# Gated attention in high and low parts: three split passes in place of fp32 products, and two output products issued earlier

## The reference, cut to what matters

```
def gla_scan(q, k, v, lg):
    def step(s, inp):
        qc, kc, vc, gc = inp
        cum = jnp.cumsum(gc, axis=1)
        qg = qc * jnp.exp(cum)
        kg = kc * jnp.exp(-cum)
        att = jnp.where(causal, jnp.einsum('blhk,bshk->bhls', qg, kg), 0.0)
        o = jnp.einsum('bhls,bshv->blhv', att, vc) + jnp.einsum('blhk,bhkv->blhv', qg, s)
        kd = kc * jnp.exp(cum[:, -1:] - cum)
        s = s * jnp.exp(cum[:, -1])[..., None] + jnp.einsum('bshk,bshv->bhkv', kd, vc)
        return s, o

    o = gla_scan(q, k, v, lg[:, :, 0]) + rev(gla_scan(rev(q), rev(k), rev(v), rev(lg[:, :, 1])))
    o = rmsnorm(o, onorm).reshape(bsz, seq, D_INNER) * jax.nn.silu(z.astype(f32))
```

## Time and profile before

| | before |
|---|---|
| median of 3 runs | 2014.81 us |
| lowest, highest | 2013.41, 2014.96 us |
| span of the profiled execution | 2012.7 us |
| mean granted clock of TensorE | 0.999 |
| busy TensorE / VectorE / ScalarE / GpSimd | 1994.2 / 1053.4 / 958.9 / 1199.7 us |
| from DRAM | 95 GB/s over the span |

### The profile page before, as it was taken

One profiled execution on the slowest core, in us unless ns is written; L12 is line 12 of the kernel. 1 busy time (PEld: TensorE's weight loads), 2 busy tenths in 40 slices (PEclk: granted clock), 3 DMA queues, 4 the chain that ended last, 5 costly groups with the idle time before them and its releaser, 6 DMA issues.

```text
span 2012.7 us, 27974 instructions
## 1 busy us (share of the span) xinstructions
PE 1994.2 (99%) x10644; PEld 1672.5 (83%) x10644; DVE 1053.4 (52%) x1576; ACT 958.9 (48%) x1641; POOL 1199.7 (60%) x955
## 2 busy tenths in 40 slices
PE   9999999999999999999999999999999999999998
PEld 7888899988877788899888779988897887777787
DVE  3184677642144436587632388778875244443321
ACT  4124445622244446355523386677675335554543
POOL 4445888875542225889865568788886442423342
PEclk9999999999999999999999999999999999999999
DMA  5233332333433312323333343434433421212131
GB/s 172 85 103 98 102 105 85 110 90 93 120 102 87 94 51 84 105 85 105 107 93 100 104 126 109 126 105 111 129 96 85 107 89 63 65 62 84 42 105 63
DMA packets 259573, 193.66 MB, mean 96 GB/s; under 512 B 9555, under 2 KB 247431, under 8 KB 259448
## 3 DMA queue, kind: packets, MB, share of 16 engines
q1 hardware_dynamic: 256188, 190.67, 31.8%
q10 hardware_dynamic: 3260, 1.28, 0.3%
HBM read 189.66 MB, written 2.27 MB: 95 GB/s over the span
## 4 chain that ended last, share of the span: by engine, by line
PE 57%; issue 23%; POOL 15%; ACT 2%; DVE 2%; DMA 1%; POOLq 0%; SPq 0%; ACTq 0%; DVEq 0%
POOL wlo L813 13%; PE bank L2624 12%; PE bank L2625 12%; PE bank L2626 12%; PE bank L2850 5%; PE bank L2851 5%; PE bank L2852 5%; PE bank L3232 1%; PE bank L3228 1%; PE bank L3196 1%; POOL f0aLo L849 1%; DMA rows<-cums 1%; DVE xc L2207 1%; POOL wlo L882 0%; DVE xC L2207 0%
## 5 line engine op out<-in xcount | busy, mean ns | idle before, releaser
L813 POOL TENSOR_TENSOR wlo<-raw,whi 128x512 fp32r<-128x512 f32 (+1 forms) x532 | 673.3, 1297 | 696.4 <-ACT whi L971 682.8
L971 ACT ACTIVATE whi<-raw 128x2048 fp32r<-128x2048 f32 (+1 forms) x131 | 233.0, 1779 | 306.9 <-PE bank L2626 298.2
L2624 PE MATMUL bank<-hHi,whi 128*128 128x512 f32 (+1 forms) x880 | 349.7, 397 | 1.0 <-DVE hLo L2535 0.9
L2626 PE MATMUL bank<-hHi,wlo 128*128 128x512 f32 (+1 forms) x880 | 341.5, 388 | 0.0
L2625 PE MATMUL bank<-hLo,whi 128*128 128x512 f32 (+1 forms) x880 | 341.2, 388 | 0.0
L2624 PE MATMUL bank<-whi,hHi 128*128 128x256 f32 (+1 forms) x640 | 219.3, 343 | 0.4 <-issue 0.3
L2626 PE MATMUL bank<-whi,hLo 128*128 128x256 f32 (+1 forms) x640 | 208.5, 326 | 0.0
L2625 PE MATMUL bank<-wlo,hHi 128*128 128x256 f32 (+1 forms) x640 | 208.3, 325 | 0.0
L834 POOL TENSOR_TENSOR wlo<-raw,whi 128x512 fp32r<-128x512 f32 x134 | 196.0, 1489 | 17.3 <-ACT whi L1138 17.3
L2624 PEld LDWEIGHTS bank<-hHi,whi 128*128 128x128 f32 x880 | 165.3, 188 | 40.8 <-issue 5.1
L2626 PEld LDWEIGHTS bank<-hHi,wlo 128*128 128x128 f32 x880 | 165.3, 188 | 34.7
(11 more groups left out here) (490 smaller groups left out, 4408.9 us busy)
## 6 DMA issues: line engine op xcount, KB each, us to landing
raw<-in_ssd_w_in SPq DMA_DIRECT2D x48, 512.0 KB, 5.0
raw<-in_ffn_w_gate SPq DMA_DIRECT2D x44, 512.0 KB, 4.8
raw<-in_ffn_w_up SPq DMA_DIRECT2D x44, 512.0 KB, 4.8
raw<-in_gla_w_in SPq DMA_DIRECT2D x40, 512.0 KB, 4.5
rows<-cums SPq DMA_DIRECT2D x64, 256.0 KB, 5.5
raw<-in_ffn_w_down SPq DMA_DIRECT2D x32, 384.0 KB, 3.4
raw<-in_attn_w_qkv SPq DMA_DIRECT2D x24, 512.0 KB, 4.3
raw<-in_conv_w_in SPq DMA_DIRECT2D x23, 512.0 KB, 4.4
```

What stands on the lines that cost most here:

```text
L813: ins = pool.tensor_tensor(wlo[s][:, part], raw[s][:, part], whi[s][:, part].bitcast(F32), ALU.subtract)
L971: act.activation(whi[s][:, 0:w], raw[s][:, 0:w], ACT.Copy).then_inc(w_hi, 1)
L2624: pe.matmul(dst, hi1, hi2, start=first, stop=False)
L2626: return pe.matmul(dst, lo1, hi2, start=False, stop=last)
```

## The change

The values, the turned keys and the attention weights are now kept as a high and a low part each, of type F32R, and their products are three split passes (`product`) instead of one fp32 product.

- Values: ScalarE's copy writes the high part `gvHi` (semaphore `gv_hi`, a used-up one under another name), and VectorE's new `value_low` subtracts it from the bank into `gvLo`; now VectorE frees the bank. There is one set of four tiles for all heads instead of two, so ScalarE's copy waits until the previous head's products have read the tile (`values_read`).
- Turned keys: ScalarE writes `kdHi0` and `kdHi1`, VectorE's new `keys_low` writes `kdLo`, and the increments wait for it (`kd_lo`).
- Attention weights: a cast to `attHi` and a subtraction into `attLo` on VectorE at the end of `attention`.
- `outs(h, 0)` goes ahead of the second half of piece 0. `outs(h, 1)` goes to the end of piece 0 in heads 1 and 2 and stays in piece 1 in heads 0 and 3. ScalarE's `keep` follows them, and VectorE's `states(h, 2)` goes to piece 0.
- `t32` has another place in memory, and the scratch for DMA descriptors is set to 1024.

```diff
--- before.py
+++ after.py
@@ -174,7 +174,8 @@
 
 LATER = {"q_hi": ("x_turn", 8), "q_lo": ("w0_lo", 3), "q_mm": ("y_mixed", 8), "s_made": ("y_hi", 8), "kept": ("x_squared", 8),
          "c_made": ("w0_hi", 1), "xg_made": ("cu_edge", 1), "t_made": ("rb_one", 1), "t_hi": ("toe_mm", 2), "t_lo": ("y_ready", 8),
-         "f_hi": ("x_in0", 16), "f_lo0": ("x_in1", 16), "f_lo1": ("x_in2", 16)}
+         "f_hi": ("x_in0", 16), "f_lo0": ("x_in1", 16), "f_lo1": ("x_in2", 16),
+         "gv_hi": ("vec_ready", 3), "kd_lo": ("vec_turned", 4)}
 
 
 STAGES = ["conv", "ffn0", "attn", "ffn1", "mid", "ssd", "gla", "end"]
@@ -262,9 +263,6 @@
         rc = sb("rc", [P, 24 * 8])
         stat = sb("stat", [P, 64])
         m_g45 = sb("g45", [P, 64])
-        t32 = [sb(f"t32_{i}", [P, SEQ]) for i in range(2)]
-
-
         @contextmanager
         def scope(spec):
             with ExitStack() as c:
@@ -275,6 +273,8 @@
                 return m
 
         R8, R4, V = [P, KT * SEQ], [P, NT * SEQ], [P, SEQ]
+        m_keys = area([(f"kdHi{d}", V, F32R) for d in range(2)])
+        t32 = [sb(f"t32_{i}", [P, SEQ]) for i in range(2)]
         m_in = area([("xtok", R8, F32), ("vrows", [P, 3 * P], F32), ("xsq", R8, F32)])
         m_conv = area([("cu", [P, KT * 514], F32), ("c0", V, F32), ("c1", V, F32), ("r2", V, F32), ("cacc", [P, 2 * SEQ], F32),
                        ("yHi", R8, F32R), ("yLo", R8, F32R)])
@@ -310,8 +310,8 @@
         with scope([("gO", [P, NT * DI], F32)]) as m_go:
             m_gl = area([("wgl4", [P, KT * P], F32R)])
             m_gla = area([("gst", [P, 6 * SEQ], F32), ("gQK", [P, 8 * SEQ], F32), ("lg", [P, 2 * SEQ], F32),
-                          ("kg", [P, 2 * SEQ], F32), ("diff", [P, 2 * SEQ], F32), ("att", V, F32), ("glT", V, F32R),
-                          ("gv0", R4, F32), ("gv1", R4, F32), ("wgf", [P, 1024], F32R),
+                          ("kg", [P, 2 * SEQ], F32), ("diff", [P, 2 * SEQ], F32), ("att", V, F32), ("attHi", V, F32R), ("attLo", V, F32R),
+                          ("glT", V, F32R), ("gvHi", R4, F32R), ("gvLo", R4, F32R), ("kdLo", [P, 2 * SEQ], F32R), ("wgf", [P, 1024], F32R),
                           ("attF", [P, P], F32), ("attB", [P, P], F32),
                           ("gdec", [P, 4 * NGC], F32), ("tdec", [P, 4 * NT], F32)])
             m_gla2 = area([("gHi", R8, F32R), ("gLo", R8, F32R)])
@@ -431,8 +431,21 @@
         def h4(ap):
             return ap.rearrange("p (h e) -> p h e", h=HPG)
 
-        def values(h, t):
-            return tile(m_gla[f"gv{h % 2}"], t)
+        def values(t):
+
+            return tile(m_gla["gvHi"], t), tile(m_gla["gvLo"], t)
+
+        def turned_keys_of(d, t):
+
+            return tile(m_keys[f"kdHi{d}"], t, P), m_gla["kdLo"][:, SEQ * d + P * t:SEQ * d + P * (t + 1)]
+
+        def attended(t):
+
+            return tile(m_gla["attHi"], t, P), tile(m_gla["attLo"], t, P)
+
+        def values_read(h, t):
+
+            return 8 * h + (2 if t in (0, NT - 1) else 4)
 
         def decayed_q(h, d):
 
@@ -1587,7 +1600,10 @@
 
                 def value_tile(h, t):
 
-                    copy(values(h, t), projected("v", h, t), S(f"side{t % 2}"), scale=rcol(5, t))
+                    v = projected("v", h, t)
+                    if h:
+                        act.wait_ge(S("go_mm"), values_read(h - 1, t))
+                    copy(values(t)[0], v, L("gv_hi"), scale=rcol(5, t))
 
                 def value_piece(h, p, half):
 
@@ -1649,7 +1665,7 @@
                 def turned_keys(h):
                     for d in range(2):
                         act.wait_ge(S("kd_turned"), 2 * h + d + 1)
-                        copy(t32[d][:, :], bank[6 + d][:, :], S("kdt_ready"))
+                        copy(m_keys[f"kdHi{d}"][:, :], bank[6 + d][:, :], S("kdt_ready"))
 
                 def keep(h, n):
 
@@ -1688,12 +1704,14 @@
                         if n == 3 and h < 3:
                             turned_keys(h + 1)
                         fill(h, n, 0)
+                        if n == 0:
+                            keep(h, 0)
                         fill(h, n, 1)
                         if h >= 2:
                             turned(h - 2, n)
-                        if n < 2:
-                            keep(h, n)
-                        else:
+                        if n == (1 if gla_piece(h, 0, 1) is None else 0):
+                            keep(h, 1)
+                        elif n >= 2:
                             squares(h, n)
                         if n == 0 and h < 3:
                             for d in range(2):
@@ -2490,7 +2508,22 @@
                         chain.note(dve.copy_predicated(m["attF"][:, :], LE[:, :].bitcast(I32), bank[4][:, P * t:P * (t + 1)]))
                         chain(dve.copy_predicated(m["attB"][:, :], GE[:, :].bitcast(I32), bank[5][:, P * t:P * (t + 1)]))
                         chain(tt(att[:, P * t:P * (t + 1)], m["attF"][:, :], m["attB"][:, :], ALU.add))
-                    dve.sem_inc(S("att_ready"), 1)
+                    chain(dve.tensor_copy(m["attHi"][:, :], att[:, :]))
+                    tt(m["attLo"][:, :], att[:, :], m["attHi"][:, :].bitcast(F32), ALU.subtract).then_inc(S("att_ready"), 1)
+
+                def value_low(h, t):
+
+                    dve.wait_ge(*late("gv_hi", 4 * h + t + 1))
+                    hi, lo = values(t)
+                    from_bank = (early_bank(t) if h == 0 else bank[t % 2])[:, :]
+                    stt3(lo, from_bank, rcol(5, t), hi.bitcast(F32), ALU.mult, ALU.subtract).then_inc(S(f"side{t % 2}"), 1)
+
+                def keys_low(h):
+
+                    for d in range(2):
+                        dve.wait_ge(S("kdt_ready"), 2 * h + d + 1)
+                        tt(m["kdLo"][:, SEQ * d:SEQ * (d + 1)], bank[6 + d][:, :], m_keys[f"kdHi{d}"][:, :].bitcast(F32),
+                           ALU.subtract).then_inc(L("kd_lo"), 1)
 
                 def states(h, n):
 
@@ -2528,6 +2561,9 @@
                     piece = gla_piece(h, n, e)
                     if piece and piece[0] == "z":
                         gate(*piece[1:])
+                    elif piece and piece[3]:
+                        for t in (2 * piece[2], 2 * piece[2] + 1):
+                            value_low(piece[1], t)
 
                 def y_low(k):
                     dve.wait_ge(S("gy_hi"), k + 1)
@@ -2542,12 +2578,12 @@
                             states(h, 1)
                             if h:
                                 head_mean(h - 1)
-                        elif n == 1:
-                            states(h, 2)
                         if n == 0 and h < 3:
                             cumulate(h + 1)
                         if n == 0 and h:
                             head_inverse(h - 1)
+                        if n == 0:
+                            states(h, 2)
                         fill(h, n, 0)
                         if n == 2 and h < 3:
                             spans(h + 1)
@@ -2557,6 +2593,8 @@
                         fill(h, n, 1)
                         if n == 1 and h < 3:
                             factors(h + 1)
+                        if n == 3 and h < 3:
+                            keys_low(h + 1)
                         if n >= 2 and (h or n == 3):
                             add(h, n)
 
@@ -2576,8 +2614,13 @@
                 q_or_k(7)
                 dve.wait_ge(S("gqk_free"), 8)
                 factors(0)
+                for t in range(2):
+                    value_low(0, t)
                 spans(0)
                 attention(0)
+                keys_low(0)
+                for t in range(2, NT):
+                    value_low(0, t)
                 for h in range(GLA_HEADS):
                     head(h)
                 head_mean(GLA_HEADS - 1)
@@ -3457,7 +3500,7 @@
                 def increments(h, n):
 
                     if n == 0:
-                        pe.wait_ge(S("kdt_ready"), 2 * h + 2)
+                        pe.wait_ge(*late("kd_lo", 2 * h + 2))
                         pe.wait_ge(S("att_ready"), h + 1)
                         for t in (2, 3):
                             pe.wait_ge(S(f"side{t % 2}"), SIDE["v", h, t][1] + 1)
@@ -3465,7 +3508,7 @@
                         pe.wait_ge(S("gla_state"), 6 * h + 2)
                     for d in range(2):
                         t = n if d == 0 else NT - 1 - n
-                        pe.matmul(bank[4 + 2 * d + n % 2][:, :], tile(t32[d], t, P), values(h, t), start=True, stop=True).then_inc(S("gu_mm"), 1)
+                        product(bank[4 + 2 * d + n % 2][:, :], *turned_keys_of(d, t), *values(t), True, True).then_inc(S("gu_mm"), 1)
 
                 def outs(h, n):
 
@@ -3479,7 +3522,7 @@
                         t = out_tile(n, d)
                         out = bank[2 + d]
                         if n < 2:
-                            ins = pe.matmul(out[:, :], m["att"][:, P * t:P * (t + 1)], values(h, t), start=True, stop=n == 0)
```

(9 more changed lines are left out.)

## The result

| | before | after |
|---|---|---|
| median of 5 runs | 2014.81 us | 2027.21 us |
| lowest, highest | 2013.41, 2015.18 us | 2026.7, 2028.29 us |
| span of the profiled execution | 2012.7 us | 2025.2 us |
| mean granted clock of TensorE | 0.999 | 0.996 |

The changed kernel is slower: the ratio is 1.0063, 95% interval 1.0051 to 1.0075. The forecast was 2026.7 us, with a range of 2019 to 2033.

What follows compares the result with a forecast made beforehand. TensorE, busy 99% of the span at full clock, was taken to bound the kernel. The passes' -7.1 and the added waits summed to +11.9 on 2012.7, span 2024.6, so 2026.7 us; range 2019 to 2033 at 0.8.

Steps and rivals of the forecast that it cites:

- The sum: All terms over the whole kernel: +11.9 us on the profiled span of 2012.7, giving 2024.6.
- Passes: On TensorE, 40 fp32 products of 0.858 become 120 passes of 0.227: 7.1 us less, 1.8 per head.
- Weight chain of head 1: TensorE waits for z's weight unit, late behind ScalarE's held copy of value tile 1: 3.5 to 4.6, taken as 4.1 us.
- Weight chain of head 2: Same chain plus one ScalarE copy, taken in two waits, 1.5 and about 2.9: together 4.4 us.
- The first part: In head 2, piece 1 waits 1.5 us for bank 0, which ScalarE's copy frees.
- Factors on VectorE: In heads 1 and 2, factor products slowed beside GpSimd's low parts make the scores late, 1.9 and 2.1; taken as 3.4 us.
- rival 1: Clock falls to 1.2 GHz in the two large waits, likelier about 2 us each: 2028 to 2033, chance 0.15.
- Tails: Between heads, VectorE's added casts and subtractions make TensorE wait: 1.3, 2.6, 0.7 and 0.8, with smaller waits at bank 0.
- Start of head 0: First increments wait for VectorE's added cast and subtractions: 1.3 us.
- Heads 1 to 2 and 2 to 3: First increments wait for the two key subtractions on VectorE: 0.7 and 0.8 us.
- turned(0, 2): In head 2, turning part 2 of head 0's outputs waits for bank 0, freed later by VectorE: 1.3 us.
- turned(0, 0): In head 2, turning part 0 of head 0's outputs waits for value tile 0's low part, behind the states: 0.3 us.

Runs made afterwards that it cites:

- e4: Changed kernel, each product of high and low parts as one fp32 matmul of the high parts, low parts made but unused: 2033.84 us, ratio 1.0097.
- e5: Changed kernel with a second pair of buffers for value tile 1 and output 1 back between the halves of the values' second piece: 2025.23 us, ratio 1.0054.
- e8: Changed kernel with ScalarE making the factors between the copies of value tiles 0 and 1 in heads 1 and 2: 2026.32 us, ratio 1.0058.
- e2: Changed kernel with VectorE's six factor products ahead of the low parts of value tiles 2 and 3 in heads 1 and 2: 2025.63 us, ratio 1.0059.
- e1: Changed kernel with 15 and 12 extra TensorE passes into unused bank 7 during the weight-unit waits of heads 1 and 2: 2026.64 us, ratio 1.006.
- e3: Changed kernel with the edits of e1 and e2 together: 2023.81 us, ratio 1.0048.
- e7: Changed kernel with the edits of e5, e6 and e2 together: 2018.9 us over 11 runs, ratio 1.0019.
- e11: e10 with the second key subtraction awaited only by the second increment, and head 2's step-2 states behind tile 0's low part: 2011.25 us, ratio 0.9984.
- e6: Changed kernel, VectorE's order between heads: attention-weight split behind key and value subtractions, key subtractions ahead of second z products in heads 1, 2: 2025.66 us, ratio 1.0053.
- e10: e7 with gate copies ahead of squares, addition ahead of split, head 2's bank-0 copy earlier, output 0 later, value tile 0 double-buffered: 2013.01 us, ratio 0.9991.

## Why the prediction came out right, and where it did not

The sum, +11.9, met +12.5 of span, and the passes and the two weight chains came in the size forecast. That it came so near is in part luck: it took 3.4 for a wait that is 0, and left out 4.4 of slow passes.

- **Passes, -7.1: right.** 0.227 apart in the products; head 3 alone gives 1.64 of its 1.78 back, and e4 prices a product at 0.18.
- **Weight chain of head 1, 4.1: right.** 3.55, by the chain counted: the held copy at 1745.13, keeps, table load, factors, high part at 1752.03, low part from 1754.01. e5 (chain taken away, wait gone) and e8 (factors taken out of it, 1.70 left, and that set by another chain) show it. VectorE's way through GpSimd's low part was a part of it: 0.43 (e2).
- **Weight chain of head 2, 4.4: size right, cause half wrong.** 1.42 + 2.81 = 4.2. The first part is as forecast. Of the second the unit makes 1.6; the rest is bank 0, which the prediction named but let be free at the same time. With output 1 ahead of turned(0, 1), nothing of TensorE's stands between this and z(1, 0) while ScalarE finishes a high part. It stands ahead of it in e5 too, which is one reason why e5 got so little.
- **Factors on VectorE, 3.4: the step that failed.** The contention was right (1.75 to 1.77 a product), the lateness too: with the clock held up the scores waited 1.67 and 1.17 (e1), against 1.9 and 2.1 (in head 3's factors only four of the six products were slow). The forecast counted with a wait of 4.6 for the unit in this step and with 4.1 in the sum; with 4.1 its own 1.9 would have been 2.4. But in the kernel after, that wait is 0. The clock fell, the first half of z took 2.7 and 1.7 longer, and the scores were wanted later. The 4.4 of rival 1 stood in the place of the 3.4, not on top: the rival's 2028 to 2033 added the two and was too high. e1 and e2, which each take one of them away, gain 0.8 and 1.8 in the two heads, and 1.1 of the 1.8 is that the clock was at half for a shorter time; e3, which takes both, gains 4.5.
- **Tails: right.** Start of head 0: 1.3 forecast, 1.75 measured, of which some 0.5 lie ahead of it (the last attention weight was done that much later). Head 0 took 41.45 where 40.69 - 1.78 would be left: 2.5 against 2.6. Heads 1 to 2 and 2 to 3: 0.55 and 0.58 against 0.7 and 0.8. turned(0, 2): 1.10 against 1.3. turned(0, 0), 0.3, has no wait.

What the chip did between VectorE and GpSimd was read from rows before and after alike. The Trainium skill, SBUF — State Buffer, "Summary: rules for kernel authors", has a VectorE instruction with two SBUF inputs and a GpSimd instruction that reads SBUF exclude each other, the second to issue waiting for the first to finish. The trace agrees: a product of 0.68 becomes one of 1.75 beside GpSimd's low parts of 1.25, and the value subtractions, which read one operand from a bank, stay at 0.75.

It stays open why the clock fell behind some of the shorter waits and not behind others (below). The spread of e7's runs, 2015.9 to 2020.8, goes with the mean granted clock of each: the four at 0.999 took 2015.9 to 2017.4, the seven at 0.998 took 2018.6 to 2020.8. So the clock fell in some and not in others, of one kernel; where it fell is not known, as only one execution of e7 was profiled, and that one had no fall in the heads. Some 2 us of the 12.5 stand in no row either: the listed waits of the heads (13.3), the slow passes (4.4) and the passes (-7.1) make 10.6, and the rest lies in what each wait costs beyond its row.

## What to carry to other kernels

When a product is moved ahead, write down what it covered at its old place on every queue: here output 1 covered a weight unit's low part, a bank's copy on ScalarE and the factors on VectorE. The lateness of the factors came up only when what stood before it was taken away, and the unit's 1.6 only when the bank's copy was. Waits in series hide each other, so price them by taking them away one by one and together; one edit alone gave 0.4 to 2.0 us of the median, which is within the intervals, and those of e11 together 16, which is not. On a TensorE this dense each of the waits of over 3 us at z(0, 0) cost its own length and 1.6 to 2.7 us of slow passes behind it, so a term for the clock belongs into the sum beside the wait, less what other engines catch up meanwhile.

## What the runs showed of the hardware

The granted clock in the profiled executions of after and of the experiments, by the wait ahead of it. It fell from 1.00 to half

- behind the waits of 3.1 to 3.6 us at z(0, 0) in five of five, and behind that of 3.07 at the scores (e5);
- behind that of 2.81 at z(1, 0) in three of seven;
- behind that of 2.26 at the scores (e8), but behind none of the six of 0.8 to 1.7 there;
- behind that of 2.0 at the start of head 1 (e6, e7) in one of two;
- behind that of 1.4 at the start of head 0 (with the gates between, some 1.6 in all) in five of eight, but behind the equally long one in piece 1 of head 2 in none of eight;
- behind the three small ones (0.9, 0.2, 0.7) at the start of head 1 in one of eight.

With the same wait at the same place it came in one execution and not in another, and what decides between them is not shown. Where a half follows, a fall can be priced by its length against 5.44: 1.5 to 3.0 us. At the start of head 0 it cost 1.5 to 1.7 (42.93 to 43.12 against 41.45 to 41.48). The Trainium skill, TensorE: Matmul & The Clock Gate, Part 1, has the clock fall by half when the array idles and come back with sustained work. The rows agree on both levels and on the direction. No fall stands in the heads before the change, where no wait was over 0.6 us, nor in e10 and e11, where none was over 1.01; but none stands in the profiled executions of e3 and e7 either, which have waits of 1.41 and of 2.81.
